# A depthwise convolution moved wholly to VectorE, spread over more of the kernel, and the branch that needs it merged last

## What is computed

```python
z = x @ w_in + b_in
q, k, v, u_sg, v_sg, glu_a, glu_g = split(z)              # each 512 wide
a  = neighbourhood_attention(q, k, v, rpb) @ w_a_o         # branch 0
u, vs = gelu(u_sg), layer_norm(gelu(v_sg))
bb = (u * (w_s @ vs + b_s)) @ w_b_o                        # branch 1
h = glu_a * sigmoid(glu_g)
h = depthwise_conv(h, conv_w, taps=31, 'SAME') + conv_b    # along the tokens
c = silu(layer_norm(h)) @ w_c_o                            # branch 2
g = sigmoid(x @ w_gate + b_gate)                           # three gates, each 1024 wide
merged = g[0] * a + g[1] * bb + g[2] * c
m = merged @ w_o + b_o
```

## Time and profile before

| what | value |
|---|---|
| time, median of 3 runs | 873.01 us (872.35 to 874.24) |
| the profiled execution, first to last instruction | 872.2 us |
| PE busy | 774.1 us (89%), 3620 matmuls |
| DVE busy | 628.1 us (72%) |
| ACT busy | 471.4 us (54%) |
| POOL busy | 192.1 us (22%) |
| DMA moved | 171.9 MB |

### The profile page before, as it was taken

One profiled execution on the slowest core, in us unless ns is written; L12 is line 12 of the kernel. 1 busy time (PEld: TensorE's weight loads), 2 busy tenths in 40 slices (PEclk: granted clock), 3 DMA queues, 4 the chain that ended last, 5 costly groups with the idle time before them and its releaser, 6 DMA issues.

```text
span 872.2 us, 11492 instructions
## 1 busy us (share of the span) xinstructions
PE 774.1 (89%) x3620; PEld 633.9 (73%) x3620; DVE 628.1 (72%) x831; ACT 471.4 (54%) x633; POOL 192.1 (22%) x151
## 2 busy tenths in 40 slices
PE   2999677799989999999999767999999999999930
PEld 2788566687778888888878656888888888888820
DVE  4589995787772523325256863999999999998958
ACT  5425544777863222422221333887888887888811
POOL 2105963763000000000101501111111211111706
PEclk9899988899999999999999976999999999999985
DMA  8734245422104233332485682999999999997252
GB/s 256 216 89 117 67 131 167 111 61 62 49 24 129 90 103 93 98 103 88 145 298 205 217 290 71 307 349 355 360 372 361 373 369 352 370 358 293 71 194 119
DMA packets 129101, 171.91 MB, mean 197 GB/s; under 512 B 15338, under 2 KB 67270, under 8 KB 129046
## 3 DMA queue, kind: packets, MB, share of 16 engines
q1 hardware_dynamic: 121440, 154.95, 52.7%
q0 software_dynamic: 6688, 15.79, 5.3%
q10 hardware_dynamic: 934, 0.69, 0.3%
HBM read 164.05 MB, written 15.97 MB: 206 GB/s over the span
## 4 chain that ended last, share of the span: by engine, by line
PE 75%; DVE 14%; DMA 4%; ACT 3%; issue 2%; POOL 1%; ACTq 0%; DVEq 0%; POOLq 0%
PE bank L1607 22%; PE bank L1608 22%; PE bank L1609 22%; DVE conv L1000 3%; DVE w_lo L936 2%; DVE conv_odd L1000 2%; PE bank L1819 2%; DMA raw<-in_w_in_dram 2%; PE bank L1809 1%; POOL conv L1503 1%; PE bank L1645 1%; PE bank L1782 1%; PE bank L1655 1%; PE bank L1834 1%; DMA w_s_in<-in_w_s_dram 1%
## 5 line engine op out<-in xcount | busy, mean ns | idle before, releaser
L936 DVE TENSOR_TENSOR w_lo<-raw,w_hi 128x1024 fp32r<-128x1024 f32 x104 | 130.8, 1265 | 120.8 <-ACT w_hi L661 119.0
L661 ACT CAST w_hi<-raw 128x1024 fp32r<-128x1024 f32 x104 | 108.0, 1047 | 83.8 <-PE bank L1609 77.7
L1607 PE MATMUL bank<-xT_hi,w_hi 128*128 128x512 f32 x352 | 142.1, 404 | 5.7 <-DVE vs L1118 5.6
L1608 PE MATMUL bank<-xT_lo,w_hi 128*128 128x512 f32 x352 | 139.8, 397 | 0.0
L1609 PE MATMUL bank<-xT_hi,w_lo 128*128 128x512 f32 x352 | 139.5, 396 | 0.0
L1607 PEld LDWEIGHTS bank<-xT_hi,w_hi 128*128 128x128 f32 x352 | 68.1, 193 | 21.5 <-issue 7.5
L1607 PE MATMUL bank<-w_hi,xgT_hi 128*128 128x512 f32 x192 | 79.4, 414 | 1.6 <-DVE xgT_lo L1348 1.6
L1608 PEld LDWEIGHTS bank<-xT_lo,w_hi 128*128 128x128 f32 x352 | 68.0, 193 | 14.5 <-issue 0.5
L1609 PEld LDWEIGHTS bank<-xT_hi,w_lo 128*128 128x128 f32 x352 | 67.8, 193 | 14.5
L1609 PE MATMUL bank<-w_hi,xgT_lo 128*128 128x512 f32 x192 | 77.2, 402 | 0.0
L1608 PE MATMUL bank<-w_lo,xgT_hi 128*128 128x512 f32 x192 | 76.9, 400 | 0.0
(11 more groups left out here) (261 smaller groups left out, 1771.1 us busy)
## 6 DMA issues: line engine op xcount, KB each, us to landing
raw_more<-in_w_e_dram SPq DMA_DIRECT2D x48, 512.0 KB, 5.8
raw<-in_w_e_dram SPq DMA_DIRECT2D x48, 512.0 KB, 6.1
raw_late<-in_w_e_dram SPq DMA_DIRECT2D x48, 512.0 KB, 6.0
raw_rows<-in_w_e_dram SPq DMA_DIRECT2D x48, 512.0 KB, 6.4
raw<-in_w_in_dram SPq DMA_DIRECT2D x28, 512.0 KB, 5.3
raw<-in_w_gate_dram SPq DMA_DIRECT2D x24, 512.0 KB, 3.8
raw<-in_w_o_dram SPq DMA_DIRECT2D x8, 512.0 KB, 3.9
x_scratch<-x_in SPq DMA_DIRECT2D x4, 512.0 KB, 6.6
```

Of the source, the lines that this page charges most:

```text
L661: act.copy(hi_slot(j), raw_slot(j)).then_inc(hi_cast, 1)
L936: dve.tensor_tensor(lo_slot(j), raw_slot(j), hi_slot(j).bitcast(F32), ALU.subtract).then_inc(lo_cast, 1)
L1607: pe.matmul(out, hi_l, hi_r, start=start, stop=False)
L1608: pe.matmul(out, hi_l, lo_r, start=False, stop=False)
```

## The change

The products on ACT, the adds on POOL and all waits on them are gone; `convolve` now covers four chunks, 128 steps: 5 in each of the units 1 to 16, and 48 more in the first half of the merge. The norm of the convolution moves into the merge, and the merge is written out: first rows 0 to 3 with branches 0 and 1 (units 28 to 51), then a pass over rows 0 to 3 with branch 2 alone (units 52 to 63, from `U_LAST`). `merged` holds all eight chunks, in the room of `mT_lo`. The squares go to the room of `conv_in`, the norm's scratch to a tile of its own, `conv_ln`.

```diff
-U_WO = U_MERGE + 36
+U_LAST = U_MERGE + 24
+U_WO = U_LAST + 12
+R_MEAN, R_VAR = 2, 3
...
-    b.use("conv_mean", 0)
-    b.use("conv_var", 1)
...
+    for r in range(4):
+        for n in range(2):
+            u = U_MERGE + 6 * r + 3 * n
+            for d in range(2):
+                b.use(("gate", r, n, d), 4 * n + d, u + d)
+            for d in range(2):
+                b.use(("branch", r, n, d), 4 * n + 2 + d, u + 2)
+            if r == R_MEAN and n == 0:
+                b.use("conv_mean", 2)
+            if r == R_VAR and n == 0:
+                b.use("conv_var", 3)
+    for r in range(4):
+        u = U_LAST + 3 * r
...
+            b.use(("gate", r, 2, d), 4 * (r % 2) + d, u + d)
...
+            b.use(("branch", r, 2, d), 4 * (r % 2) + 2 + d, u + 2)
```

ACT, in the merge (`open_gate` waits for the gate's bank and applies the sigmoid; `merged_hi_rows` rounds two merged chunks):

```diff
-        def product(c, k):
...
+        for r in range(4):
+            for n in range(2):
+                u = U_MERGE + 6 * r + 3 * n
+                cast_hi(u + 2)
+                open_gate(r, n, 0)
+                cast_hi(u + 3)
+                open_gate(r, n, 1)
+                cast_hi(u + 4)
+                if r == R_MEAN and n == 1:
...
+                        act.activation(squares[c], conv[:, c, :], ACT.Square).then_inc(squared, 1)
+                if r == R_VAR and n == 1:
+                    act.wait_ge(*drained("conv_var"))
+                    act.activation(conv_rstd, conv_vare, ACT.Sqrt).then_inc(conv_root, 1)
+        for r in range(4):
+            u = U_LAST + 3 * r
+            cast_hi(u + 2)
+            open_gate(r, 2, 0)
+            if r == 0:
+                for c in range(WC):
+                    act.wait_ge(conv_scaled, c + 1)
+                    act.activation(conv[:, c, :], conv[:, c, :], ACT.Silu, bias=column(V_CVB + c),
+                                   scale=column(V_CVG + c)).then_inc(conv_silu, 1)
+                for c in range(WC):
+                    act.wait_ge(conv_silu, c + 1)
+                    act.copy(branch_hi[2][:, c, :], conv[:, c, :]).then_inc(conv_hi, 1)
+            else:
+                merged_hi_rows(r - 1)
+            cast_hi(u + 3)
+            open_gate(r, 2, 1)
+            cast_hi(u + 4)
+        merged_hi_rows(3)
```

DVE (`weigh` multiplies a branch by its gate, two chunks, and for n > 0 adds; `centre`, `variance` and `scale_conv` hold the same instructions as before):

```diff
-            if u < U_V:
-                convolve(5 * (u - 1) if u else 0, 5 * u)
-            elif u < 16:
-                convolve(35 + 4 * (u - 8), 35 + 4 * (u - 7))
+            if 1 <= u <= 16:
+                convolve(5 * (u - 1), 5 * u)
...
+        done = 80
+        for r in range(4):
+            for n in range(2):
+                u = U_MERGE + 6 * r + 3 * n
+                cast_lo(u + 2)
+                convolve(done, done + 4)
+                done += 4
+                if r == R_MEAN and n == 1:
+                    centre()
+                cast_lo(u + 3)
+                convolve(done, done + 4)
+                done += 4
+                if r == R_VAR and n == 1:
+                    variance()
+                cast_lo(u + 4)
...
+                weigh(r, n)
+                convolve(done, done + 4)
+                done += 4
+                if r == R_VAR and n == 1:
+                    scale_conv()
+        for r in range(4):
+            u = U_LAST + 3 * r
+            cast_lo(u + 2)
+            if r == 0:
+                for c in range(WC):
+                    dve.wait_ge(conv_hi, c + 1)
...
+            cast_lo(u + 3)
+            if r:
+                merged_lo_rows(r - 1)
+            cast_lo(u + 4)
+            weigh(r, 2)
+        merged_lo_rows(3)
```

POOL, and PE's order in the merge:

```diff
-        for c in (WC - 1, WC - 2):
-            for k in range(1, TAPS):
...
-                pool.tensor_tensor(conv[:, c, :], conv[:, c, :], products[c][:, k % 2, :], ALU.add).then_inc(
-                    pool_conv, 1)
...
-        pool.wait_ge(unit_used, U_WO - 3)
+        pool.wait_ge(unit_used, U_WO - 1)
...
+        for r in range(4):
+            merge(U_MERGE + 6 * r, r, 0)
+            if r == R_MEAN:
+                conv_mean()
+            if r == R_VAR:
+                conv_var()
+            merge(U_MERGE + 6 * r + 3, r, 1)
+        for r in range(4):
+            merge(U_LAST + 3 * r, r, 2)
```

More of the change, by code:

```diff
@@ L120, in plan_banks @@
         b.use(("spatial", c), 6 + c % 2)
-    b.use("conv_mean", 0)
-    b.use("conv_var", 1)
-    uses = []
-    for r in range(2):
+    for r in range(4):
[11 more added lines that the diff above has]
+        u = U_LAST + 3 * r
         for d in range(2):
[L126 to L129, removed]
+            b.use(("gate", r, 2, d), 4 * (r % 2) + d, u + d)
+        for d in range(2):
+            b.use(("branch", r, 2, d), 4 * (r % 2) + 2 + d, u + 2)
     for n in range(2):
@@ L785, in _ @@
                                bias=column(V_IN + 12 + c)).then_inc(frees(("usg", c)), 1)
[L788 to L819, removed]
@@ new lines, in open_gate @@
+        def open_gate(r, n, d):
+            if n < 2 and r:
+                act.wait_ge(*drained(("branch", r - 1, n, d)))
+            elif n == 2 and r < 2:
+                act.wait_ge(*drained(("branch", 3, r, d)))
+            elif n == 2:
+                act.wait_ge(*drained(("branch", r - 2, 2, d)))
+            name = ("gate", r, n, d)
+            act.wait_ge(*filled(name))
+            act.activation(gate[:, n if n < 2 else r % 2, d, :], bank(name)[:], ACT.Sigmoid,
+                           bias=column(V_GATE + n * DC + 2 * r + d)).then_inc(frees(name), 1)
@@ L1181, in _, with centre, variance @@
-        steps[:] = base + 8, 0, None
+        def centre():
+            dve.wait_ge(*filled("conv_mean"))
+            for c in range(WC):
+                dve.scalar_tensor_tensor(out=conv[:, c, :], in0=bank("conv_mean")[:], scalar=-1.0 / W,
+                                         in1=conv[:, c, :], op0=ALU.mult, op1=ALU.add).then_inc(centred, 1)
+            dve.wait_ge(centred, WC)
+            dve.sem_inc(frees("conv_mean"), 1)
+        def variance():
+            dve.wait_ge(*filled("conv_var"))
+            dve.tensor_scalar(conv_vare, bank("conv_var")[:], 1.0 / W, EPS, ALU.mult, ALU.add).then_inc(
+                frees("conv_var"), 1)
@@ new lines, in weigh @@
+        def weigh(r, n):
+            for d in range(2):
+                name = ("branch", r, n, d)
+                dve.wait_ge(*filled(name))
+                dve.wait_ge(*drained(("gate", r, n, d)))
+                out = part[:, d, :] if n else merged[:, 2 * r + d, :]
+                dve.tensor_tensor(out, gate[:, n if n < 2 else r % 2, d, :], bank(name)[:], ALU.mult).then_inc(
+                    frees(name), 1)
+            for d in range(2 if n else 0):
+                row = merged[:, 2 * r + d, :]
+                dve.wait_ge(*drained(("branch", r, 0, d)))
+                dve.wait_ge(*drained(("branch", r, n, d)))
+                o = dve.tensor_tensor(row, row, part[:, d, :], ALU.add)
+                if n == 1:
+                    o.then_inc(dve_step, 1)
+                    step()
+                else:
+                    o.then_inc(merged_ready, 1)
@@ new lines, in conv_var, with merge @@
+        def conv_var():
+            open_bank("conv_var")
+            for c in range(WC):
+                pe.wait_ge(squared, c + 1)
+                o = pe.matmul(bank("conv_var")[:], ones, squares[c], start=c == 0, stop=c == WC - 1)
+            o.then_inc(fills("conv_var"), 1)
+        def merge(u, r, n):
+            for d in range(2):
+                features(u + d, [("gate", r, n, d)], xT_hi, xT_lo)
+            if n == 0:
+                pe.wait_ge(*drained(("attended", 7)))
+            elif n == 1:
+                pe.wait_ge(gated_lo, WC)
+            else:
+                pe.wait_ge(conv_lo, WC)
+            features(u + 2, [("branch", r, n, d) for d in range(2)], branch_hi[n], branch_lo[n])
```

198 lines of the change are left out of this document (58 added, 140 removed).

## The result

| | before | changed |
|---|---|---|
| median of 4 runs | 873.4 us (872.35 to 874.24) | 848.11 us (847.02 to 848.94) |
| span of the profiled execution | 872.2 us | 847.0 us |

The ratio is 0.9712, 95% interval 0.9696 to 0.9727: 25.3 us less, where 28 were predicted, and 848.1 lies in the range of 840 to 855 and in the forecast's own of 841 to 849.

What follows compares the result with a forecast made beforehand. PE waits for DVE, whose two-input steps take 1.68 instead of 0.66 us while POOL adds. w_o starts at 421.5 instead of 449.42: 872.2 - 27.9 + 0.8 = 845.1, said as 845; own range 841 to 849, whole range 840 to 855.

Steps and rivals of the forecast that it cites:

- The step: DVE's convolution step: 0.66 us with POOL quiet, about 1.68 while POOL adds; a low cast 1.14 with POOL quiet.
- rival (3): Long steps come from the place in the kernel, not POOL; 1.68 stays, about 950 us, slower; chance 0.03.
- Units 8 to 16: Units 8 to 15 take 43.5 us from 70.58; after a bank wait of 1.1, unit 16 starts at 115.2, not 136.26.
- The v windows: v store issued at 93.1, load 19 landing at 127.1, first transpose of probabilities at 141, bad end 143.6.
- Rival (1): Landing of load 19 or the chain to the first transpose does not follow DVE: 847 to 857 us; chance 0.15.
- To the merge: First transpose to unit 28: 80.6 us less a 2.7 wait, 1.75 of clock and 6.9 of matmuls; unit 28 at 210.2.
- Mean and variance: In the merge, their matmuls add 6.9 us, and DVE's reading of banks 2 and 3 adds 2.8 together.
- The norm: Ahead of the last pass, PE waits 3.8 us, plus 1.75 of clock; the wait could be 0 to 5.6.
- The merge's steps: 48 convolution steps lie under the merge: DVE needs 13.8 us per three-unit group, PE 16.3.
- Behind w_o: After w_o starts, the late residual request is priced at nothing, at worst 3 us; the rest is counted as equal.
- Unrolling: Writing out the merge loop: the jump costs at most 2.0 us, nothing in the sum; some might be gained on top.

Runs made afterwards that it cites:

- e1: The changed kernel with 60 two-input adds of 128x512 on POOL, over an idle buffer, from unit 8 on: 894.07 us in one run.
- e6: The changed kernel with mean and variance of the convolution in PSUM banks 6 and 7 instead of 2 and 3: 846.68 us, ratio 0.9689.
- e11: The changed kernel run once more, unedited, in five rounds: 848.61 us, ratio 0.9725.
- e7: The changed kernel with the norm of the convolution done in units 49 to 51: 842.5 us, ratio 0.9643.
- e4: The kernel before with its two-iteration merge loop written out, nothing else: 872.61 us, ratio 0.9999.
- e5: The changed kernel with the merge's 48 convolution steps done in units 17 to 26 instead, 5 a unit: 873.22 us, ratio 0.9998.
- e9: The changed kernel with 20 convolution steps moved from the merge to units 17 to 26, two a unit: 856.12 us, ratio 0.9806.
- e12: The changed kernel with 12 convolution steps moved from the merge to units 20 to 25, two a unit: 851.61 us, ratio 0.9747.

## Why the prediction was right

By its own steps:

- **The step.** 0.66 and 1.14 were taken from the stretch with POOL quiet, and hold everywhere; rival (3) is out. e1 brings 1.68 and 2.2 back with POOL's adds alone, so the factor of two and a half is the step's; the low cast's is 1.9.
- **Units 8 to 16.** 115.2 predicted, 115.04 measured, with the one bank wait (1.1; measured 1.02).
- **The v windows.** Store at 93.1 (measured 93.8), load 19 landing at 127.1 (127.6), first transpose at 141 (140.89). The 141 was a choice: the sum of the chain gave 143.6, and PE's own readiness 141 to 143. From the landing to the transpose it took 13.3 us instead of 20.9; the masks gave back 4.2 of these 7.6, and the rest, for which the prediction had no row, came too. Rival (1) is out.
- **To the merge.** Unit 28 at 210.2, measured 210.19. That it fits to the hundredth is luck. The prediction took the whole wait of 2.7 away, and 0.8 of it stayed (in unit 26). Against that it had booked one clock loss, of 1.75, where the kernel before had two: 1.7 behind the first scores and 1.1 behind the wait of unit 27.
- **Mean and variance.** 6.9 for the matmuls and 2.8 for two banks, 9.7. Measured: PE would have gone on at 291.9 and at 329.1 (starts of the groups before, plus 16.3), and lost 1.0 and 1.5 by the waits. Mean and variance themselves cost 3.6 each: the next group starts 3.1 behind their first matmul and lasts 0.4 longer than 16.3. That is 9.7 in all, and e6 shows the 2.8 by itself.
- **The norm.** The wait, predicted 3.8 and measured 3.96 (4.1 with the tail of the matmul before it), was right, and so were the chain's parts: scales end at 361.3, silu at 362.5, the low parts begin at 363.02. The clock behind it was priced at 1.75, the loss behind one wait of 3.34, and this is not a fixed price: it cost 7.91 - 5.44 = 2.5 in the first profiled execution and 1.8 in e11's. Together 6.6 or 5.9 instead of 5.5, and e7 gains 6.4. That e11's loss meets the 1.75 is no proof of the price.
- **The merge's steps.** No wait from them: the 65 us from 228 hold 47.3 of DVE's work. The three groups of the last pass took 16.5 each instead of 16.3, 0.5 more together; w_o came at 422.98, not 421.5 (422.19 in e11).
- **Behind w_o.** Counted as equal, it is 1.2 us longer: 424.0 from w_o to the end, against 422.8. The residual was there in time (436.66, without a wait), as priced. The eight w_o units took 44.5 instead of 44.1, with the DMA share at 0.88 instead of 0.73, and the transposes behind them ran slower. The other profiles agree: e4, with the old order of the merge, has 422.7, and e5 to e9, e11 and e12 have 423.7 to 424.9, so it belongs to the change. Whether it is the residual's late transfers was not tried, and stays open.
- **Unrolling.** Priced at nothing, and e4 measured nothing.
- **Rival (3), its sum.** Its 25 us more for units 8 to 16 should be 21: these nine took 74 us before (70.58 to 144.57), against its 95. Nothing else hangs on it.

In spans, 25.2 were gained of the forecast 27.9: 1.5 are lost up to w_o, 1.2 behind it. The prediction added 0.8 between span and median. In the runs since, an execution's time lies 1.8 to 2.0 over its own span, so the profiled execution of before was probably the slowest of its three (874.24), and the 0.8 said nothing of the changed one.

## What to carry to other kernels

Look for instructions of GpSimd that read SBUF beside VectorE's two-input ones before counting GpSimd's time as free: here 60 adds and the products that fed them, with ACT and POOL far from full, cost 30 us, and taking the work back to the fuller engine gained 25. Whether a step on VectorE is free is decided by what stands behind it in VectorE's order, not by the idle time that a window shows. It was free in units 8 to 15, 20 to 24 and in the merge, where the work behind it had time to spare. In units 17, 18 and 25, ahead of the chain that PE waits for, it cost nearly its whole length, and clock on top. Work that is moved under a long stretch of matmuls still needs its last chain (here a norm over five engine changes) started early enough, here two units earlier, and an accumulator bank that nobody is still reading.

## What the runs showed that was not expected

- A POOL memset that reads nothing leaves DVE's two-input steps at 0.66, but stretches its one-input TENSOR_SCALARs from 0.54 and 0.48 to 1.01 and 1.25 us.
- DVE's hold-up goes by POOL's instructions, not by their length: a one-input one of 128x1024, 2.77 us and more, holds one DVE instruction up by 0.78; a two-input one of 128x512, 1.6 long, holds one up by 1.0.
- The clock lost behind a wait is not one price, not even for the same kernel at the same place. Behind a wait of 3.96 or 3.97 ahead of unit 54, that unit took 7.1 to 8.4 us in nine profiled executions, against 5.44 at the full clock, and 7.26 and 7.91 in the two of the changed kernel. At the first scores, unit 20 took its usual 8.52 after a wait of 1.99 in e6, and 10.10 after only 1.26 in e7. So differences of 1 or 2 us between two profiles can be the clock's alone, and need the medians beside them.
